# Fourteen early expert blocks multiplied in split halves, two late blocks instead of twenty, and the scaled rows' low part on VectorE

## The reference

```python
def peer_ffn(h, peer_wq, sub_keys1, sub_keys2, peer_u, peer_v):
    q = (h @ peer_wq).reshape(B, T, PEER_HEADS, PEER_QDIM)
    ...
    v1, i1 = lax.top_k(s1, PEER_TOPK)
    v2, i2 = lax.top_k(s2, PEER_TOPK)
    ...
    top_s, pos = lax.top_k(cand_s, PEER_TOPK)
    eid = jnp.take_along_axis(cand_i, pos, axis=-1)
    gate = jax.nn.softmax(top_s, axis=-1)
    ...
        a = jnp.einsum('td,tkd->tk', hb, peer_u[eb], preferred_element_type=jnp.float32)
        a = jax.nn.gelu(a, approximate=False)
        return jnp.einsum('tk,tkd->td', (gb * a).astype(hb.dtype), peer_v[eb])
```

## Time and profile before

| what | value |
|---|---|
| time, median of 3 runs (lowest, highest) | 942.15 us (941.81, 942.99) |
| the profiled execution: its own time, its span | 940.36 us, 938.6 us |
| TensorE busy | 932.3 us, 99% of the span |
| VectorE, ScalarE, GpSimd busy | 765.6, 500.3, 322.7 us |
| granted TensorE clock | 1.00 of full speed throughout |
| DMA | 193.46 MB, mean 206 GB/s |

### The profile page before, as it was taken

One profiled execution on the slowest core, in us unless ns is written; L12 is line 12 of the kernel. 1 busy time (PEld: TensorE's weight loads), 2 busy tenths in 40 slices (PEclk: granted clock), 3 DMA queues, 4 the chain that ended last, 5 costly groups with the idle time before them and its releaser, 6 DMA issues.

```text
span 938.6 us, 15372 instructions
## 1 busy us (share of the span) xinstructions
PE 932.3 (99%) x5396; PEld 816.9 (87%) x5396; DVE 765.6 (82%) x1450; ACT 500.3 (53%) x872; POOL 322.7 (34%) x292
## 2 busy tenths in 40 slices
PE   9999999999999999999999999999999999999998
PEld 9998899998988888888888888888888888888887
DVE  6899758999886888778778898888888888777776
ACT  6576544433777777777777543433334343343442
POOL 3084228887576766767667000000000000000000
PEclk9999999999999999999999999999999999999999
DMA  9543239826776676767667877777777777666664
GB/s 295 159 135 116 66 95 307 216 62 194 218 238 200 207 219 189 233 205 223 202 194 225 264 238 247 233 246 238 240 242 238 242 237 245 207 216 188 193 192 142
DMA packets 93782, 193.46 MB, mean 206 GB/s; under 512 B 8448, under 2 KB 59264, under 8 KB 93456
## 3 DMA queue, kind: packets, MB, share of 16 engines
q1 hardware_dynamic: 93280, 190.38, 64.9%
q0 software_dynamic: 288, 2.10, 1.2%
q10 hardware_dynamic: 144, 0.08, 0.0%
HBM read 174.43 MB, written 15.99 MB: 203 GB/s over the span
## 4 chain that ended last, share of the span: by engine, by line
PE 97%; ACT 1%; DVE 1%; DMA 0%; issue 0%; DVEq 0%; ACTq 0%
PE psum L2143 37%; PE psum L2063 17%; PE psum L2060 9%; PE psum L1682 5%; PE psum L1985 5%; PE psum L1954 4%; PE psum L2123 4%; PE psum L2089 3%; PE psum L2057 3%; PE psum L1698 3%; PE psum L2126 2%; PE psum L1739 1%; PE psum L1863 1%; PE psum L1979 1%; PE psum L1946 1%; DMA cst<-in_const_dram 0%
## 5 line engine op out<-in xcount | busy, mean ns | idle before, releaser
L2143 PE MATMUL psum<-rr 128*128 128x512 f32 x1536 | 354.1, 391 | 0.0
L2143 PEld LDWEIGHTS psum<-rr 128*128 128x128 f32 x1536 | 286.1, 188 | 63.5
L856 ACT ACTIVATE rr<-raw 128x1024 fp32r<-128x1024 f32 x105 | 111.7, 1064 | 176.0 <-PE psum L2143 175.9
L1337 DVE TENSOR_TENSOR rr<-raw,rr 128x1024 fp32r<-128x1024 f32 x106 | 129.9, 1225 | 26.0 <-ACT rr L856 25.6
L2063 PE MATMUL psum<-h_all,rr 128*128 128x512 f32 x456 | 123.3, 395 | 0.0
L2063 PEld LDWEIGHTS psum<-h_all,rr 128*128 128x128 f32 x456 | 82.5, 188 | 13.5
L1357 DVE TENSOR_REDUCE gel<-psum 128x256 f32<-128x512 f32 x86 | 58.7, 683 | 13.4 <-DMA up_kept<-gel 10.9
L764 ACT ACTIVATE rr<-raw 128x1024 fp32r<-128x1024 f32 x64 | 67.3, 1051 | 3.3 <-DMA raw<-in_peer_u_dram 3.3
L2063 PE MATMUL psum<-h_all,late_b 128*128 128x512 f32 x232 | 64.8, 394 | 0.0
L1642 POOL TENSOR_TENSOR rr<-raw,h_all 128x640 fp32r<-128x640 bf16 x32 | 40.3, 1259 | 56.3 <-DVE raw L1314 53.7
L1405 DVE TENSOR_TENSOR rr<-big,rr 128x256 fp32r<-128x256 f32 x128 | 54.5, 426 | 4.4
(11 more groups left out here) (242 smaller groups left out, 1763.4 us busy)
## 6 DMA issues: line engine op xcount, KB each, us to landing
raw<-in_peer_v_dram SPq DMA_DIRECT2D x128, 512.0 KB, 3.9
raw<-in_peer_u_dram SPq DMA_DIRECT2D x127, 512.0 KB, 4.2
up_kept<-gel SPq DMA_DIRECT2D x106, 128.0 KB, 3.6
gel<-up_kept SPq DMA_DIRECT2D x106, 128.0 KB, 3.9
big<-in_w_in_dram SPq DMA_DIRECT2D x10, 1024.0 KB, 5.8
big<-in_peer_wq_dram SPq DMA_DIRECT2D x8, 1024.0 KB, 5.5
big<-in_w_out_dram SPq DMA_DIRECT2D x4, 1024.0 KB, 5.1
rr<-big POOLq DMA_DIRECT2D x2, 1024.0 KB, 8.9
```

Of the source, the lines that this page charges most:

```text
L856: act.activation(v_sp[b % 2][:, 0, :], early_v(b), ACT.Copy).then_inc(v_hi, 1)
L1337: dve.tensor_tensor(v_sp[b % 2][:, 1, :], early_v(b), f(v_sp[b % 2][:, 0, :]), ALU.subtract).then_inc(v_lo, 1)
L2143: i = pe.matmul(psum[:, 4 + 2 * t + n, :], g_sp[:, s, x, t * P:(t + 1) * P], v_sp[s][:, y, n * 512:(n + 1) * 512], start=(first and m == 0 ...
```

## The change

- `EARLY` goes from 108 to 126, so that 18 more blocks have their up-product early and only two late; the loops of all engines go.
- Of the early blocks the plain ones are now 0 to 8 (before 0 to 12); 9 to 21 are split blocks ahead of the picks (before none), 22 is the one that the turning of the picks interrupts (before 13), 23 to 125 fill the gate stage (before 14 to 107).
- The high and low parts of blocks 9 to 19 are put between the last steps of the search on ScalarE and VectorE. A split block ahead of the fill waits for the Gelu two blocks back. Their raw data comes through three more buffers (`raw_more`) for blocks 9 to 11, loaded once the last query is multiplied.
- The scaled rows' high part moves ahead on ScalarE, and their low part is one operation on VectorE, between two steps of the search, in place of four on GpSimd.
- In the mixer the first of the six Relu operations moves from ScalarE to VectorE, and the logits are taken up after two heads, no longer three.
- The final residual rows are fetched to other places, and the raw buffers of V keep a ring of three to the end.

```diff
-EARLY, EARLY_TOP = 108, 15
-RING_END = EARLY - 1 - (EARLY - 2) % 3
+EARLY, EARLY_TOP = 126, 24
+SPLIT0 = PH + 1
...
-EXP_AT = EARLY_TOP - 5
+EXP_AT = SPLIT0 + 7
...
             def keep_early(e):
                 sp.wait_ge(e_up, e + 1)
-                load_ring(e + 3)
+                if e < SPLIT0 - 3:
+                    load_ring(e + 3)
+                else:
+                    sp.wait_ge(ld_t[e % 3], 16 * (e // 3 + 2))
+                    load_ring(e + 6)
                 if e:
                     store_early(e - 1)
+                if e in (SPLIT0 - 5, SPLIT0 - 4):
+                    sp.wait_ge(z_done, z_after(N_CHUNK - 1))
+                    for n in ((SPLIT0, SPLIT0 + 1) if e == SPLIT0 - 5 else (SPLIT0 + 2,)):
...
+                        load_ring(n)
...
-                act.wait_ge(pe_sc, g + 1)
-                for t in range(2):
+                act.wait_ge(*((pe_sc, g + 1) if g else (d_relu, 1)))
+                for t in range(g == 0, 2):
...
+                if h == PH - 1:
+                    act.wait_ge(p_t32, 1)
+                    act.activation(ht[:, 0], t32s, ACT.Copy).then_inc(a_hi, 1)
...
+            early_high(SPLIT0)
+            early_high(SPLIT0 + 1)
+            early_gelu(PH - 1)
+            early_high(SPLIT0 + 2)
             numbers(PH - 1)
-            for e in range(PH - 1, EXP_AT):
+            for e in range(PH, EXP_AT):
                 early_gelu(e)
+                if e < SPLIT0 + 2:
+                    early_high(e + 4)
+                elif e >= SPLIT0 + 4:
+                    early_high(e + 2)
             act.wait_ge(d_sub, 1)
             act.activation(pick3[:, 2], pick3[:, 2], ACT.Exp).then_inc(a_soft, 1)
             early_gelu(EXP_AT)
             act.wait_ge(a_iota, 1)
             act.activation(psum[:, 0, 0:NK], numbers_sb, ACT.Copy).then_inc(a_iota, 1)
+            early_high(EXP_AT + 2)
...
-            logits(0, 0, 3)
-            logits(1, 0, 3)
+            logits(0, 0, 2)
+            logits(1, 0, 2)
...
             for h in range(PH + 1):
...
+                if h == PH - 1:
+                    early_low(SPLIT0)
                 if h < PH:
                     best_keys(h)
+                if h == PH - 1:
+                    early_low(SPLIT0 + 1)
...
                 if h >= 2:
                     best_pairs(h - 1)
+                if h == PH - 2:
+                    dve.wait_ge(a_hi, 4)
+                    dve.tensor_tensor(ht[:, 1], t32s, f(ht[:, 0]), ALU.subtract).then_inc(d_hlo, 1)
+                if h == PH - 1:
+                    early_low(SPLIT0 + 2)
                 if h == PH:
+                    early_low(SPLIT0 + 6)
                     dve.tensor_tensor(pick3[:, 2], vtop, vtop[:, :, :, 0:1].to_broadcast([P, 2, PH, TOPK]), ALU.subtract).then_inc(d_sub, 1)
                     last_matches()
+                    early_low(SPLIT0 + 7)
                 if h >= 2:
                     look_up(h - 2)
-
+                if h == PH - 1:
+                    for e in range(SPLIT0 + 3, SPLIT0 + 6):
+                        early_low(e)
+
+            early_low(SPLIT0 + 8)
+            early_low(SPLIT0 + 9)
             dve.wait_ge(d_seq, seq.n)
             look_up(PH - 1)
+            early_low(SPLIT0 + 10)
...
-            def low_part(n):
-                pool.wait_ge(a_hi, 4)
-                ks = slice(2 * n, 2 * n + 2)
-                pool.tensor_tensor(ht[:, 1, ks, :], t32s[:, ks, :], f(ht[:, 0, ks, :]), ALU.subtract).then_inc(p_hlo, 1)
...
-            for e in range(PH - 2, EARLY_TOP - 2):
+            for e in range(PH - 2, SPLIT0):
                 early_up(e)
...
+                        if e < FILL0:
+                            pe.wait_ge(e_gel, e - 1)
...
-            pe.wait_ge(e_gel, EARLY_TOP - 3)
             pe.wait_ge(a_hi, 4)
-            pe.wait_ge(p_hlo, N_OUT)
+            for e in range(SPLIT0, SPLIT_E[0]):
+                split_part(e, 0, UNITS)
             split_part(SPLIT_E[0], 0, 2 * DK)
...
-            with pe.Fori(EARLY // 2 + 1, NK // 2 - 1) as i:
-                pe.wait_ge(a_gel, 2 * i + (1 - EARLY))
-                up(0, 2 * i + 2)
-                down(0, 2 * i, False, False)
```

223 lines of the change are left out of this document (74 added, 149 removed).

## The result

The changed kernel took 942.84 us (median of 14 runs), the kernel before 941.91 (14 runs): a ratio of 1.0016, with a 95% interval of 1.0009 to 1.0024. It is slower by 0.16%; the forecast was 942.1 and no change.

What follows compares the result with a forecast made beforehand. The prediction took TensorE's matmul work to bound the kernel. Work -1.65, mended waits -0.4 and new split-stage waits +2.0 summed to 0.0 on the median of 942.15, so 942.1 us, range 939.8 to 944.1.

Steps and rivals of the forecast that it cites:

- What bounds the kernel: Whole kernel: TensorE works 932.3 of 938.6 us, so only matmul work and new waits move the time.
- Matmul work: TensorE: four plain blocks become split ones, 18 up-products leave the loop; -2.46 and +0.8, together -1.65 us.
- Mended waits: Mixer: Relu moved to VectorE and logits after two heads take off 0.1 and 0.3, together -0.4 us; bounds 0 and -1.0.
- The moved low part: Scaled rows' low part on VectorE, 2.29 us where VectorE would wait anyway: costs the path about nothing.
- New waits in the split stage: TensorE waits for high and low parts near blocks 16 to 20: +2.0 us, between 1.0 and 3.6.
- first chain: From block 15's end, ScalarE 6.0 then VectorE 8.8 us: block 20's low part comes 1.6 us late.
- second chain: VectorE low parts meet GpSimd products: 1.3 us in hand at block 17; with two met, 1.8 late.
- What is left hidden: Down stage: VectorE stays hidden, V's block 3 lands with about 1.5 us in hand; cover lost would cost about 1.
- The sum: Whole kernel: -1.65 - 0.4 + 2.0 = 0.0, so the median of 942.15 stays at 942.1 us.
- the one that would be slower: Split stage: port collisions and late loads in SyncE's queue add up, waits of 4.0 us or more, 944.7; chance 0.14.

Runs made afterwards that it cites:

- e12: Changed kernel with the edits of e2, e5, e6, e9, e10, e11, and in blocks 12 to 19 loads ahead of stores: 939.90 us, 0.9986 of the kernel before.
- e1: The changed kernel again, unedited, for a second profile: 942.68 us, 1.0010 of the kernel before.
- e9: Changed kernel with VectorE's low part of block 19 ahead of head 7's look-up and of block 20 ahead of the closing operations: 941.52 us, 1.0006 of the kernel before.
- e15: Kernel before with only the mixer's two mends (first Relu on VectorE, logits after two heads): the mixer's stretch took 198.83 us, as before.
- e8: Changed kernel with the scaled rows' low part given back to GpSimd in four operations: 942.73 us, 1.0007 of the kernel before.
- e4: Changed kernel with the loads of V's block 3 and the first late block of U issued as early as before the change: 942.24 us, 1.0004.
- e5: Changed kernel with ScalarE's second last early Gelu ahead of its copy of V's block 1: 943.60 us, 1.0009 of the kernel before.
- e11: Changed kernel with e5's Gelu order, V's block 3 loaded early as in e4, and both late U blocks fetched later, inside the down stage: 941.50 us, 1.0001.
- e2: Changed kernel with the store of block 5's Gelu issued ahead of SyncE's wait for load 8: 942.57 us, 1.0008 of the kernel before.
- e3: Changed kernel with ScalarE's copy of block 18's high part ahead of the Exp and its table loads: 942.51 us, 1.0009 of the kernel before.
- e6: Changed kernel with ScalarE's copy of block 17's high part ahead of the Gelu of block 15: 942.74 us, 1.0007 of the kernel before.
- e10: Changed kernel with the loads of blocks 9 to 11 waiting only for the last two queries' weights to be split: 942.54 us, 1.0012 of the kernel before.
- e13: The kernel before again, unedited, for a second profile: span 939.4 us.
- e14: The kernel before again, unedited, for a third profile: span 939.4 us.
- e7: Changed kernel with the edits of e2, e4, e5 and e6 together: 941.58 us, 0.9997 of the kernel before.

## Why the prediction was wrong

**What bounds the kernel** and the prices held: plain blocks, split blocks, the dense down stage (320.66 / 1404 x 12 = 2.741 a block) and the gate stage (320.57, forecast 321.0).

**Matmul work, -1.65**: right, or a little small. The shortest of each stretch that a variant showed (49.5 in e12, 320.57 in e1, 359.0 in e9, where the down stage starts at 579.78 of 938.7) make 729.1; before they were 731.3 at their shortest, so -2.2.

**Mended waits, -0.4**: mis-sized; e15 measures 0.0. The prediction saw the next waits behind both, but gave 0.1 and 0.3 for what lay between.

**The moved low part, 0**: right, and for the reason given (e8).

**New waits in the split stage, +2.0**: this step failed. Over pure work the stage took 5.4 us in the first profile, 3.2 in e1, 3.1 in e4, e5 and e8, 2.0 in e11, 3.3 in the mean of these six, which don't touch it or, e8, don't change it. Counting single starts from block 9 gives the start of block 16, which is the end of block 15, where the prediction's first chain (ScalarE, then VectorE) begins:

| profile | block 9 later than 10.36 us after block 6 | VectorE's low part of 12 took | block 16 late by | from there to block 20's last third | stage over pure work |
|---|---|---|---|---|---|
| first | 2.2 | 2.58 | 3.6 | 14.97 | 5.4 |
| e1 | 0.5 | 2.60 | 1.4 | 14.98 | 3.2 |
| e5 | 0.1 | 2.62 | 1.3 | 14.97 | 3.1 |
| e11 | 0.3 | 1.21 | 0.2 | 14.96 | 2.0 |

The first chain was right, in place and in size: the prediction has 6.0 + 8.8 = 14.8 us for it, pure work takes 13.25, so it costs 1.7 each time, which TensorE waits at blocks 17 to 20 (e9 takes the waits at 19 and 20 away). Wrong is how the rest was put together with it. The prediction let the chain's start move only by a part of the other lateness; but that lateness arose ahead of block 15, and the whole of it adds.

Its second chain came as forecast, too: two GpSimd products were met, by the low parts of 12 and 15 (2.60 and 2.61 us in e1). But the prediction held VectorE's list against TensorE at block 17 alone, with 1.3 in hand. At block 12 there is 0.1 in hand: in e2, where GpSimd waited, the low part ended 20.7 us after block 6, and TensorE wants it 10.36 + 8.52 + 1.89 = 20.8 after. So the collision cost TensorE its time at block 12, and block 17 was left with 0.3. No edit kept the two engines apart there; that the collision is the cause is read from these rows and from e2 and e11, where GpSimd waited instead.

What was not in the prediction at all is SyncE's queue: TensorE was let to block 9 at 217.6 without asking what its Gelu waits for. Block 9 needs Gelu 7, that needs a store landed, and the store stands behind SyncE's wait for a load and behind further loads. This decided the first profile, e3, e6 and e9 (waits of 1.6 to 2.0), where Gelu 7 came 6.2 to 6.4 us after that store's issue, against 4.6 to 4.9 in e1, e4, e5, e8 and e11. In e1 it cost nothing of its own: the low part of 12 came 22.0 to 22.1 us after block 6 in e1, e4, e5, e8 and e10, whether block 9 had waited 0.3 or not at all.

**What is left hidden**: this step failed too. The load of V's block 3 is hidden, as said. But the copy of V's block 1 was not looked at: it waits for its own load ahead of the last Gelus, and before the change that load landed in time. Loads of V took 3.9 in the median; this one took 7.13. From the turning to the end of the span the forecast is 680.7; the eight profiles without an edit of the down stage (first, e1 to e3, e6, e8 to e10) have 680.0 to 684.0, 681.9 in the mean: +1.2. In e11, without a wait there, it was 679.6.

**The sum**: on e1 the misses are 0.4 (mends), 1.2 (split stage) and 0.2 (behind the turning), less 0.3 for the launch, 1.5 in all; e1's span of 940.5 lies 1.4 over the mean of before's three (939.1), and the measured ratio is +1.5 us. The base of the sum was fair: e13 and e14 are 0.8 longer than the profile it was made on, mostly by launch and gate stage. That the sum missed by no more is in part luck: the matmul work gave some 0.5 more than counted, which hides as much of the waits. Of the rivals, the one that would be slower named the collisions and SyncE's queue, but the loads behind late low parts, not a store behind loads; its 4.0 us of waits were reached, of the six, in the first profile alone. What stays open is why that store took 1.6 us longer in some executions than in others, and the load of V's block 1 7.1 us in the first profile and 5.9 in e8, and what decides which of two engines waits at the low part of 12.

## What to carry to other kernels

When an early stage is speeded up, follow each matmul's wait back through the buffers to the queue: a result that must be stored before its buffer is free hangs on everything queued ahead of the store, and a queue that waits for a landing holds all that stand behind. When a list of work feeds another engine, hold it against that engine at every step that takes from it, not at the last alone; and two late chains run side by side only if neither starts from a step that the other delays. A copy that waits for a load, ahead of a short operation that the critical engine needs, is a wait that only shows when the load is slow; put the short one first. A mended wait counts only if the next thing asked of the same engine comes earlier too.

## What the runs showed of the hardware

A busy stretch behind an idle one ran slow once. In the first profile TensorE was nearly idle from 217.0 to 219.3, and then its granted clock fell (window, its length, busy us and instructions of TensorE, its weight loads, VectorE, ScalarE and GpSimd, granted clock, DMA share, GB/s):

```profile
219.30:223.40 4.10, 4.06 (x21) 4.09 (x22) 3.98 (x21) 2.39 (x5) 3.66 (x14) 0.58 0.38 143
223.40:245.00 21.60, 21.60 (x186) 21.60 (x185) 18.30 (x31) 10.18 (x15) 9.58 (x10) 1.00 0.52 165
```

A mean of 0.58 of full speed is mostly the lower of the two levels, 1.2 of 2.4 GHz; 21 matmuls took 4.1 us, which at the second row's rate (21.6 / 186) take 2.4: the wait of 2.0 cost 1.7 more. e7's wait of 2.1 and e3's of 1.7 had no such stretch, so what brings it stays open.

VectorE and GpSimd held each other up in both directions: VectorE's low part took 2.92 us in e7 and 2.60 in e1 instead of 1.2, GpSimd's sum 2.74 in e1 instead of 1.89, and its half product 4.93 instead of 1.55 behind three low parts in e2. Which of them waits is not told by the recorded starts: at the low part of 12 GpSimd's start stands 0.04 us ahead in e1 (226.63 and 226.67), where VectorE waited, and in e2 (226.95 and 226.99), where GpSimd did. The Trainium skill (SBUF — State Buffer, section Who interferes with whom) has the exclusion for the whole instruction; these rows agree.

A small store landed late behind large loads: 6.35 us for 128 KB behind loads of 512 KB, where the median of all 124 stores is 3.5.
